# Six weight chunks kept in SBUF: a smaller descriptor ring, half the queries, and a few instructions moved

## The reference

```python
def mixer_conformer(y, w_pw1, b_pw1, conv_w, conv_b, ln_g, ln_b, w_pw2, b_pw2):
    z = y @ w_pw1 + b_pw1
    a, g = jnp.split(z, 2, axis=-1)
    z = a * jax.nn.sigmoid(g)
    z = causal_depthwise_conv(z, conv_w) + conv_b
    z = jax.nn.silu(layernorm(z, ln_g, ln_b))
    return z @ w_pw2 + b_pw2

def peer(y, w_q, sub_keys, u, v):
    ...
    q = (yt @ w_q).reshape(T, PEER_HEADS, 2, PEER_HALF)
    s = jnp.einsum('thpc,pnc->thpn', q, sub_keys).astype(jnp.float32)
    val, idx = lax.top_k(s, PEER_TOPK)
    cand = val[:, :, 0, :, None] + val[:, :, 1, None, :]
    ...
    top_val, top_pos = lax.top_k(cand.reshape(T, PEER_HEADS, PEER_TOPK * PEER_TOPK), PEER_TOPK)
    ...
        act = gb * jax.nn.gelu(jnp.einsum('thkd,td->thk', ub, xb), approximate=False)
        vb = jnp.take(v, eb, axis=0)
        return jnp.einsum('thk,thkd->td', act, vb)

for i in range(DEPTH):
    h = h + mixer(rmsnorm(h, mix_norm_g[i]))
    h = h + peer(rmsnorm(h, ffn_norm_g[i]), peer_w_q[i], peer_sub_keys[i], peer_u[i], peer_v[i])
```

## Time and profile before

| | us |
|---|---|
| median of 3 runs (lowest, highest) | 1625.91 (1624.79, 1631.22) |
| profiled execution, its own time | 1626.37 |
| span of its profile | 1624.6 |
| PE busy | 1046.7 (64%) |
| DVE busy | 1113.1 (69%) |
| ACT busy | 462.3 (28%) |
| POOL busy | 502.6 (31%) |
| DMA, 649.84 MB | 400 GB/s over the span |

### The profile page before, as it was taken

One profiled execution on the slowest core, in us unless ns is written; L12 is line 12 of the kernel. 1 busy time (PEld: TensorE's weight loads), 2 busy tenths in 40 slices (PEclk: granted clock), 3 DMA queues, 4 the chain that ended last, 5 costly groups with the idle time before them and its releaser, 6 DMA issues.

```text
span 1624.6 us, 19989 instructions
## 1 busy us (share of the span) xinstructions
PE 1046.7 (64%) x6936; PEld 712.2 (44%) x6936; DVE 1113.1 (69%) x3119; ACT 462.3 (28%) x953; POOL 502.6 (31%) x541
## 2 busy tenths in 40 slices
PE   8996876747644476867573477776576444544454
PEld 8995643525411265756451165655364111211111
DVE  3446768675577765987756765897756777777764
ACT  4101544111011235743121134763222111111110
POOL 0012334322233322333313322332323333333330
PEclk9997868868855799888796579887897566666655
DMA  9969999999999999899999999899999999999994
GB/s 371 355 230 380 417 411 408 419 421 417 418 422 421 421 418 417 352 421 407 420 416 421 421 419 417 353 409 394 415 418 405 422 422 422 421 422 422 421 421 194
DMA packets 106164, 649.84 MB, mean 400 GB/s; under 512 B 11728, under 2 KB 15824, under 8 KB 38480
## 3 DMA queue, kind: packets, MB, share of 16 engines
q0 software_dynamic: 76032, 553.68, 82.4%
q1 hardware_dynamic: 26400, 92.81, 14.7%
q10 hardware_dynamic: 3632, 2.08, 0.4%
...
## 4 chain that ended last, share of the span: by engine, by line
DMA 40%; PE 26%; DVE 16%; POOL 5%; ACT 5%; issue 5%; DVEq 2%; POOLq 0%; ACTq 0%
DMA ring<-in_uv_dram,expert 33%; PE ps L668 13%; DMA wring<-in_wall_dram 8%; DVE ring L1197 7%; PE ps L845 7%; POOL ring L391 5%; ACT side L569 2%; PE ps L858 2%; DVE side L1252 2%; PE ps L675 1%; ACT L460 1%; PE ps L833 1%; DVE picked L1189 1%; DVE mix L1213 1%; PE ps L886 1%
## 5 line engine op out<-in xcount | busy, mean ns | idle before, releaser
L1197 DVE CUSTOM_DVE_ANT_0 ring<-ring,ps 128x1024 f32<-128x1024 f32 x528 | 635.2, 1219 | 321.2 <-DMA ring<-in_uv_dram,expert 250.8
L391 POOL DMA_INDIRECT ring<-in_uv_dram,expert x528 | 500.5, 948 | 1086.6 <-PE ps L845 840.0
L845 PE MATMUL ps<-ring,mix 128*32 128x512 f32 x2112 | 365.6, 827 | 311.4 <-DVE mix L1213 311.2
L845 PEld LDWEIGHTS ps<-ring,mix 128*32 128x32 f32 x2112 | 67.4, 134 | 509.7 <-DVE mix L1213 367.8
L668 PE MATMUL ps<-yT,wring 128*128 128x128 f32 (+1 forms) x1472 | 205.6, 301 | 71.8 <-DMA wring<-in_wall_dram 43.7
L642 ACT ACTIVATE gel<-dots 128x4 f32<-128x4 f32 x132 | 27.1, 205 | 739.2 <-DVE dots L1197 738.8
L668 PEld LDWEIGHTS ps<-yT,wring 128*128 128x128 f32 x1472 | 193.6, 207 | 94.6 <-DMA wring<-in_wall_dram 48.1
L858 PE MATMUL ps<-sel,osb 128*128 128x16 f32 x528 | 84.0, 304 | 78.6 <-ACT osb L628 78.6
L858 PEld LDWEIGHTS ps<-sel,osb 128*128 128x128 f32 x528 | 80.6, 241 | 116.7 <-ACT osb L628 116.7
L569 ACT ACTIVATE side<-ident,params 128x128 f32<-128x128 f32 x310 | 96.5, 389 | 16.0 <-PE ps L886 14.8
L833 PE MATMUL ps<-ident,yg 128*128 128x128 f32 x264 | 49.1, 348 | 71.6 <-DVE dots L1197 71.6
...
## 6 DMA issues: line engine op xcount, KB each, us to landing
...
ring<-in_uv_dram,expert POOLq DMA_INDIRECT x528, 16.3
...
```

Of the source, the lines that this page charges most:

```text
L391: pool.indirect_dma_start(out=ring[:, i % R, :], out_offset=None, in_=uv, in_offset=bass.IndirectOffsetOnAxis(ap=expert[:, n % 2, k:k + 1] ...
L845: mm = pe.matmul(po[32 * j:32 * j + 32, half, :], mix[:, k, :], ring[:, slot, D + 512 * half:D + 512 * (half + 1)], start=(q == 0), stop=( ...
L1197: nc.vector.tensor_tensor_reduce(out=row, in0=row, in1=yrep, scale=1.0, scalar=0.0, op0=ALU.mult, op1=ALU.add, accum_out=dots[:, k:k + 1]) ...
```

## The change

1. `kept`, six chunk buffers more (24 KB a partition). The room comes from the descriptor scratch (4,096 bytes a partition), from `qT`, which now holds the queries of one half of a layer (8 or 9 groups, indexed by `query(n)`), and from one array `pairs` in the place of `cand`, `cand2` and `hot`.
2. The first 70 entries of the stream have 26 buffers, so that inB 16 to 21 are loaded into `kept` among the early ones. The six buffers then take the chunks 0 to 5 of layer 1's pw1, behind qB 15 in the stream, and both blocks use them: the stream has 170 entries.
3. Since `qT` is half as large, a half's queries may be written only when all scores of the half before are taken: qB moves to u = 23 to 26, q1 to v = 23 to 26, each with a wait on s_sc at its first copy.
4. On ACT `gates(0)` comes behind `front(-4)` and not behind `front(-1)`.
5. The first 20 diagonals of each block's conv are made at v = 0 and not at v = 6.

```diff
@@ -18,6 +18,7 @@
 NB = 4
+KEEP = 6
 R = 12
@@ -57,6 +58,10 @@
+    def query(n):
+        return n - max(b for b in (0, GF, G0, G0 + GA - 1) if b <= n)
@@ -79,7 +84,7 @@
     for k in range(16):
-        FRONT.setdefault(21 + min(k // 3, 4), []).append(("qB", k))
+        FRONT.setdefault(23 + k // 4, []).append(("qB", k))
@@ -105,17 +110,26 @@
+    for k in range(KEEP):
+        LOADED[JOB["pw10", k]] = LOADED[JOB["pw11", k]] = len(STREAM)
+        STREAM.append((48 + k, JOB["pw11", k]))
     for w in range(2):
...
             for k in range(count):
-                LOADED[JOB[name % w, k]] = len(STREAM)
-                STREAM.append((row + k, JOB[name % w, k]))
+                if JOB[name % w, k] not in LOADED:
+                    LOADED[JOB[name % w, k]] = len(STREAM)
+                    STREAM.append((row + k, JOB[name % w, k]))
     FREE = 4
-    EARLY = LOADED[JOB["inB", 15]] + 1
-    BUFFER = [(i - EARLY) % (NB + 16) if i < EARLY else (i - EARLY) % NB for i in range(len(STREAM))]
+    EARLY = LOADED[JOB["inB", 15 + KEEP]] + 1
+    HELD = [LOADED[JOB["pw10", k]] for k in range(KEEP)]
+    BUFFER = [(i - EARLY) % (NB + 16 + KEEP) for i in range(EARLY)]
+    for i in range(EARLY, len(STREAM)):
+        BUFFER.append(NB + 16 + HELD.index(i) if i in HELD else (i - EARLY - sum(j < i for j in HELD)) % NB)
     BEFORE = [[j for j in range(i) if BUFFER[j] == BUFFER[i]] for i in range(len(STREAM))]
-    assert all(BUFFER[LOADED[JOB["inB", k]]] == NB + k for k in range(16))
+    assert all(BUFFER[LOADED[JOB["inB", k]]] == NB + k for k in range(16 + KEEP))
@@ -146,9 +160,10 @@
         wring = sb("wring", [P, NB, C, P])
+        kept = sb("kept", [P, KEEP, C, P])
         hT = sb("hT", [P, C, L])
         yT = sb("yT", [P, C, L])
-        qT = sb("qT", [P, 2, NG, H, GT])
+        qT = sb("qT", [P, 2, NG - GF, H, GT])
         params = sb("params", [P, NPAR])
@@ -165,13 +180,11 @@
         rest = sb("rest", [P, 2, NK])
-        cand = sb("cand", [P, TOPK, TOPK])
-        cand2 = sb("cand2", [P, TOPK, TOPK])
+        pairs = sb("pairs", [P, 2, TOPK, TOPK])
         topv = sb("topv", [P, TOPK])
...
         posf = sb("posf", [P, 2, TOPK])
-        hot = sb("hot", [P, 2, TOPK, TOPK])
         picked = sb("picked", [P, 2, TOPK])
@@ -239,6 +252,8 @@
                 return wring[:, b, :, :]
+            if b >= NB + 16:
+                return kept[:, b - NB - 16, :, :]
             return flat[:, (4 + b) * D:(5 + b) * D].rearrange("p (c n) -> p c n", n=P)
@@ -260,7 +275,7 @@
         s_par = sem("s_par")
-        s_w = [sem(f"s_w{b}") for b in range(NB + 16)]
+        s_w = [sem(f"s_w{b}") for b in range(NB + 16 + KEEP)]
         s_par2 = sem("s_par2")
@@ -515,7 +530,10 @@
                         act.wait_ge(s_proj, m + 1)
-                        act.copy(qT[:, k % 2, GF:NG, k // 2, :], ps[:, m % 2, 0:TB].rearrange("p (g t) -> p g t", t=GT)
+                        if k == 0:
+                            act.wait_ge(s_sc, GF)
+                        act.copy(qT[:, k % 2, :, k // 2, :], ps[:, m % 2, 0:TB].rearrange("p (g t) -> p g t", t=GT)
                                  ).then_inc(s_bank[m % 2], 1)
@@ -529,9 +547,10 @@
             rows(0)
-            for u in range(-4, 0):
+            front(-4)
+            gates(0)
+            for u in range(-3, 0):
                 front(u)
-            gates(0)
@@ -560,8 +579,10 @@
                         act.sem_inc(s_ga, 1)
-                if 6 <= v < 14:
-                    for i in range(20 * (v - 6), min(20 * (v - 5), len(TAPS))):
+                if v == 0 or 7 <= v < 14:
+                    u = max(v - 6, 0)
+                    for i in range(NDIAG * u, min(NDIAG * (u + 1), len(TAPS))):
                         c, k = TAPS[i]
@@ -602,11 +623,13 @@
                     act.sem_inc(s_bank[m % 2], 1)
-                if 22 <= v < 26:
-                    for k in range(4 * (v - 22), 4 * (v - 21)):
+                if 23 <= v < 27:
+                    for k in range(4 * (v - 23), 4 * (v - 22)):
                         m = JOB["q1%d" % w, k]
                         act.wait_ge(s_proj, m + 1)
-                        act.copy(qT[:, k % 2, o0 // GT:o0 // GT + 8, k // 2, :],
+                        if k == 0:
+                            act.wait_ge(s_sc, G0 + w * (GA - 1))
+                        act.copy(qT[:, k % 2, 0:8, k // 2, :],
                                  ps[:, m % 2, 0:P].rearrange("p (g t) -> p g t", t=GT)).then_inc(s_bank[m % 2], 1)
@@ -821,7 +844,7 @@
                 for s in range(2):
-                    last = pe.matmul(psc[:, s * NK:(s + 1) * NK], qT[:, s, place(n), :, :].rearrange("p h t -> p (h t)"),
+                    last = pe.matmul(psc[:, s * NK:(s + 1) * NK], qT[:, s, query(n), :, :].rearrange("p h t -> p (h t)"),
                                      keysT[:, 2 * layer_of(n) + s, :], start=True, stop=True)
@@ -1131,8 +1154,9 @@
             sc = [psc[:, s * NK:(s + 1) * NK] for s in range(2)]
-            c1 = cand[:, :, :].rearrange("p a b -> p (a b)")
-            c2 = cand2[:, :, :].rearrange("p a b -> p (a b)")
+            cand = pairs[:, 0, :, :]
+            c1, c2 = (pairs[:, i, :, :].rearrange("p a b -> p (a b)") for i in range(2))
+            hot = pairs
@@ -1155,7 +1179,7 @@
                     nc.vector.max_index(idx[:, s, 8:16], val[:, s, 8:16], rest[:, s, :])
-                nc.vector.tensor_tensor(cand[:, :, :], val[:, 0, :].unsqueeze(2).to_broadcast([P, TOPK, TOPK]),
+                nc.vector.tensor_tensor(cand, val[:, 0, :].unsqueeze(2).to_broadcast([P, TOPK, TOPK]),
                                         val[:, 1, :].unsqueeze(1).to_broadcast([P, TOPK, TOPK]), ALU.add)
@@ -1383,7 +1407,7 @@
-    nc = _bacc.Bacc("TRN2", target_bir_lowering=False, num_devices=1)
+    nc = _bacc.Bacc("TRN2", target_bir_lowering=False, num_devices=1, dynamic_dma_scratch_size=4096)
     arrays, args = {}, []
```

## The result

| | before | after |
|---|---|---|
| median of the runs (lowest, highest), us | 1625.47 (1624.79, 1631.22) | 1609.26 (1606.77, 1610.70) |
| profiled execution, its own time and span, us | 1626.37, 1624.6 | 1606.77, 1605.0 |

The ratio of after to before is 0.9895, with a 95% interval of 0.9878 to 0.9911: 16.2 us faster by the medians, 19.6 in the two spans, since the profiled execution of after is the fastest of its four. The median stands 5.3 us above the forecast of 1604 and within the range of 1595 to 1615, but not in the 1600 to 1607 that the prediction called its forecast: it stands between that and rival A's 1612, in rival B's 1608 to 1610.

A forecast was written before the change was run, and what follows sets the result against it. Transfers, full at about 421 GB/s, were taken as the bound. Gains of 1.8 + 2.5 + 7.5 + 5 + 5.5 = 22.3 us took 1626.4 to 1604.1, median 1604; forecast 1600 to 1607, range 1595 to 1615.

The forecast's parts named there:

- rival A: Engines become the bound in both pw1 stretches, so the kept chunks bring less: 14.3 us gained, 1612; chance 0.17.
- rival B: Conv holes stay open because the diagonals behind each Gelu set POOL's next issue: 1608 to 1610; chance 0.14.
- The bound: Whole kernel: transfers at about 421 GB/s are full; time is gained only by fewer bytes there or closed holes.
- Part 1: Front: inB 16 to 21 loaded before the first gather, out of 160 to 200 us; 1.8 us, bounds 0 to 7.4.
- Part 2: Front: gates(0) earlier on ACT, hiding DVE's wait for the first exponent; 2.5 us, bounds 1.5 and 4.
- Part 3: Layer 1's pw1: six kept chunks not loaded again in the second block; 7.5 us, bounds 4 and 7.5.
- the first block gets 0: First block: kept loads cost 7.5 us in groups 6 to 8 and give 7.5 back in pw1, net 0.
- The limit of the Trainium skill: HBM limit near 358 GB/s a core; by it the six kept chunks would be worth 8.8 us.
- Part 4: Conv: first 20 diagonals at quarter 0 instead of 6 close transfer holes; 5 us in block one, 5.5 in two.
- From 659.3 to about 654, where the queue runs dry: First block's conv: POOL's next issue comes some 5 us earlier, at the time the gather queue empties.
- Part 5: Moved queries, shared array and smaller descriptor ring: 0 us, with 6 as the far end for the queries' waits.
- Rival D: Smaller descriptor ring empties at each wrap, 5.6 us a stop, 396/W more stops: slower; 0.06 with other slower ways.

The follow-up runs named there:

- e2: The changed kernel without the six early inB chunks, the kept pw1 chunks left in: 1616.68 us.
- c_after: The changed kernel measured and traced again without an edit: 1616.18 us, ratio to before 0.9895.
- g: The kernel before with only the first gates moved forward, behind the first prefetch group: 1622.62 us, ratio 0.9986.
- e4: The changed kernel with the six buffers holding early chunks only, pw1 loaded in both blocks: 1620.59 us.
- first pair: The first traces of the kernel before and the changed kernel, neither edited: spans 1624.6 and 1605.0 us.
- second pair: Traces of the kernel before and the changed kernel taken again, neither edited: spans 1627.5 and 1617.1 us.
- v3: The changed kernel keeping pw1 chunks 6, 7, 10, 11, 14, 15, loaded behind layer 1's second outB chunk: 1607.12 us, ratio 0.9881.
- v1: The changed kernel keeping pw1 chunks 6, 7, 10, 11, 14 and 15 instead of 0 to 5: 1619.35 us, ratio 0.9909.
- e3: The changed kernel with each block's first conv diagonals back at v = 6: 1623.43 us.

## Why the prediction was right, and what its terms were off by

**The bound.** Right: the earlier trace rows read as bytes and holes. The windows without a hole stay at 414 to 424 GB/s after the change, with 3.1 MB less to move.

**Part 1** (1.8, bounds 0 to 7.4): 0.5 by the medians of e2 and c_after, 3.1 by the spans; the times allow nearly anything in the bounds (1.7, give or take 5.3, by the means). The reading behind it, that a full rate at 180 us is no proof that bytes bind there, held in c_after: against e2, 7.9 us of idle time went before 140 us and 7.3 came back before 260, where the prediction had 5.7. In the first trace of after none came back (5.4 against e2's 6.3).

**Part 2** (2.5): 2.3 alone (0.8 to 3.9). Coef was forecast for 141.5; it stands at 141.18 in after and 141.05 in g. This part is shown by itself, size and mechanism.

**Part 3** (7.5 in the second block, 0 in the first): a term that was mis-sized. Undoing the keeping costs 4.4 us by the medians, which their doubt of 5.8 can't tell from 7.5; the traces show what is missing. The failed step is "the first block gets 0: 7.5 us later in groups 6 to 8, 7.5 back in pw1". The 7.5 later came (7.8 and 8.5), but in pw1 only part came back: 4.1 and 2.1 us more are idle there in the two blocks of after than of before, 3.2 and 1.9 in c_after. Rival A had named the place, "the quarters that lose their loads", with 4.5 and 3.5. So its mechanism is there, at 0.6 to 0.8 of its price (5.1 and 6.2 of 8.0 us). By e4's row groups the first block costs some 2 us net, and the second gives 6.5 of the 7.5. What I missed in the earlier trace rows is the first quarter: a sum of PE's waits over 70 us says that the whole stretch can shrink by 7.5, not that the quarter can that loses all its loads. There it is not PE's wait for chunks that counts, but POOL's 15.3 us without a free slot, which loads used to cover. The limit of the Trainium skill that the prediction weighed here (DMA: Bandwidth & Descriptors, Specifications) is passed by the windows without a hole after too (414 to 424 GB/s in those printed here).

**Part 4** (5 and 5.5, together 10.5): in the first pair 10.5 us of idle time in the conv went, just so (13.5 to 3.0), and POOL's pause before it is as forecast:

```profile
647.93 0.94 POOL L406 DMA_INDIRECT ring<-in_uv_dram,expert  x1 [9.93 <-PE ps L868]
```

In the second pair 4.0 went (10.2 to 6.2); undoing it cost 3.8 there (6.2 to 10.0), 7.3 by the medians. So the mechanism is right, and its size was between 4 and 10.5 in these traces. The 10.5 "just so" is in part luck: in the same trace 6.2 us more are idle in pw1. With pw1 full, the early diagonals leave the conv 14.1 us idle in v3, and 7.5 and 6.0 in e4 and v1. "From 659.3 to about 654, where the queue runs dry" took the gathers ahead of the pause as given; v3 shows that the pause ahead of it counts as well, for two of 11.3 and 9.4 us in a row empty the queue where one of 9.9 didn't. That is rival B's outcome, in some executions. Its mechanism, the diagonals behind the Gelu, can be read in c_after:

```profile
638.21 3.03 ACT L590 ACTIVATE side<-ident,params 128x128 f32<-128x128 f32 x10 [0.73 <-PE ps L909]
643.79 1.00 ACT L651 COPY osb<-ps 128x1024 f32<-128x1024 f32 x1
644.84 3.60 PE L881 MATMUL ps<-sel,osb 128*128 128x16 f32 x16 [4.71 <-ACT osb L651]
```

The last of the second twenty end at 641.2, the copy of `po` stands behind them, and PE waits 4.7 us for it, where before had 6.91 and after has 2.63; POOL's pause is 12.9 us. No run moved these diagonals, so what they cost is not shown. And by e3's row groups against c_after's the early diagonals are worth nothing in the first block and 4.2 us in the second, where 5 and 5.5 were forecast.

**Part 5** (0): the queries 0.3 us, the ring 0.1, both with intervals that hold no change and reach 0.14% at most. The one array for `cand`, `cand2` and `hot` was not tried by itself. Rival D's stops exist, but two and not 396/W with W near 50, and each beside a full queue: the error in its price was to take a stop of POOL for a stop of the transfers. Against D the prediction said that the trace before shows no stop of POOL with slots free; it has the one of 2.03 us. By the 16 bytes a descriptor of the Trainium skill (DMA: Bandwidth & Descriptors, Terms) the ring holds 28 gathers, an estimate; the traces have 272 between the two stops.

**Sum.** The single parts by the medians are 0.5 + 2.3 + 4.4 + 7.3 = 14.5 us, with 5 us of doubt on three of the four; 16.2 were measured, 22.3 forecast. By the balance, the stretches of parts 1 and 2 (to 260 us) gained 8.3 us in the first pair and 3.7 in the second, where 4.3 were forecast, and those of parts 3 and 4 (bytes, pw1 and conv) 11.8 and 6.4, where 18.0 were. So what is missing is in parts 3 and 4, which brought a third to two thirds of their 18; in the first pair the front covered 4.0 us of it, which is luck. How the shortfall in the median divides between the two parts can't be told from these runs.
